# A two-layer block on one core: part of the RWKV chunks' transposes taken from products with the identity to TensorE's transpose mode

## The reference, cut to what matters

```python
def step(state, inp):
    r_t, w_t, k_t, v_t, kk_t, a_t = inp
    sa = jnp.einsum('bhij,bhj->bhi', state, -kk_t)
    state = (state * w_t[:, :, None, :]
             + sa[..., None] * (kk_t * a_t)[:, :, None, :]
             + v_t[..., None] * k_t[:, :, None, :])
    y_t = jnp.einsum('bhij,bhj->bhi', state, r_t)
    return state, y_t
_, ys = lax.scan(step, state0, xs)
```

## Time and profile before

| | before |
|---|---|
| median of 3 runs | 3451.0 us (3441.01 to 3458.84) |
| the profiled execution | 3451.66 us, its span 3449.9 us |
| TensorE matmul busy | 2585.6 us (75%), 17662 instructions |
| VectorE busy | 2055.5 us (60%) |
| GpSimd busy | 1353.6 us (39%) |
| ScalarE busy | 662.9 us (19%) |
| mean granted TensorE clock | 0.869 |
| HBM | 291 GB/s over the span |

### The profile page before, as it was taken

How to read it: one execution, slowest core, us unless ns; L and a number is a source line. 1 busy time by engine, 2 the same in 40 slices (tenths; PEclk the granted TensorE clock), 3 DMA queues, 4 the chain that set the end, 5 groups by cost and what they waited for, 6 DMA issues and landing times. The chain is left out here.

```text
span 3449.9 us, 44587 instructions
## 1 busy us (share of the span) xinstructions
PE 2585.6 (75%) x17662; PEld 1854.1 (54%) x17662; DVE 2055.5 (60%) x3910; ACT 662.9 (19%) x1414; POOL 1353.6 (39%) x1094
## 2 busy tenths in 40 slices
PE   6878563674887086888865657799999887977877
PEld 5767452562332075677753436477888676322222
DVE  6446989888764878999977987425232543000001
ACT  1122002211111013132222300132323422000001
POOL 0001476687877766777754666300000110000001
PEclk8989785886999597899987878999999898999998
DMA  8617798899999998999987799632343436999997
GB/s 332 207 37 244 251 324 301 305 385 352 343 369 401 390 340 313 329 399 398 398 337 275 262 362 354 219 98 87 114 118 95 147 113 231 426 428 428 428 429 302
DMA packets 391245, 1006.30 MB, mean 292 GB/s; under 512 B 30621, under 2 KB 234755, under 8 KB 375939
## 3 DMA queue, kind: packets, MB, share of 16 engines
q0 software_dynamic: 150912, 549.52, 42.4%
q1 hardware_dynamic: 207808, 405.44, 31.8%
q10 hardware_dynamic: 32323, 48.60, 3.9%
HBM read 971.99 MB, written 31.46 MB: 291 GB/s over the span
## 5 line engine op out<-in xcount | busy, mean ns | idle before, releaser
L1615 POOL DMA_INDIRECT ring<-in_peer_u_dram,index x512 | 691.6, 1351 | 338.6 <-DVE ring L1687 159.0
L1615 POOL DMA_INDIRECT ring<-in_peer_v_dram,index x512 | 613.1, 1197 | 274.6 <-issue 131.9
L352 PE MATMUL bank<-hT,weights 128*128 128x256 f32 x1984 | 448.4, 390 | 96.7 <-DVEq L149 46.6
L352 PEld LDWEIGHTS bank<-hT,weights 128*128 128x128 f32 x1984 | 387.7, 196 | 156.6 <-issue 99.8
L2008 PE MATMUL bank<-hT,weights 128*128 128x256 f32 x1792 | 424.6, 392 | 3.8 <-DVE weights L2211 3.3
L2008 PEld LDWEIGHTS bank<-hT,weights 128*128 128x128 f32 x1792 | 339.3, 194 | 55.2 <-DVE weights L2211 3.7
L1693 DVE SCALAR_TENSOR_TENSOR h_rows_b<-ring,coef,h_rows_b 128x1024 f32<-128x1024 f32 x238 | 305.2, 1282 | 50.4 <-DMA ring<-in_peer_v_dram,index 32.0
L1687 DVE SCALAR_TENSOR_TENSOR ring<-ring,h_rows_a 128x1024 f32<-128x1024 f32 x256 | 304.9, 1222 | 44.1 <-DMA ring<-in_peer_u_dram,index 41.5
L1687 DVE SCALAR_TENSOR_TENSOR ring<-ring,h_rows_b 128x1024 f32<-128x1024 f32 x256 | 299.9, 1223 | 8.1 <-DMA ring<-in_peer_u_dram,index 7.6
L1706 PE MATMUL bank<-ring,weights 128*128 128x512 f32 x512 | 239.2, 613 | 76.4 <-ACT weights L1728 50.2
L2797 POOL TENSOR_TENSOR sd_inn<-sd_inn,ssd_y 128x1024 f32<-128x1024 f32 x8 | 18.8, 2356 | 577.8 <-ACT sd_inn L2909 577.8
(11 more groups left out here) (579 smaller groups left out, 3965.2 us busy)
## 6 DMA issues: line engine op xcount, KB each, us to landing
weights<-in_w_in_dram SPq DMA_DIRECT2D x112, 512.0 KB, 4.1
weights<-in_w_in_dram SPq DMA_DIRECT2D x54, 1024.0 KB, 10.9
xp_near<-in_w_exp_gate_dram SPq DMA_DIRECT2D x9, 4096.0 KB, 34.4
xp_far<-in_w_exp_up_dram SPq DMA_DIRECT2D x9, 4096.0 KB, 32.9
xp_near<-in_w_exp_up_dram SPq DMA_DIRECT2D x7, 4096.0 KB, 33.9
xp_far<-in_w_exp_gate_dram SPq DMA_DIRECT2D x7, 4096.0 KB, 35.7
xp_far<-in_w_exp_down_dram SPq DMA_DIRECT2D x7, 4096.0 KB, 34.4
xp_near<-in_w_exp_down_dram SPq DMA_DIRECT2D x6, 4096.0 KB, 34.5
```

The lines of the kernel that those rows point to most:

```text
L352: ins = pe.matmul(m.ps[b][:, 0:TH], m.weights[:, s, k, c * P:(c + 1) * P], rhs(k), start=(k == 0), stop=(k == k_tiles - 1))
L1615: pool.indirect_dma_start(out=self.ring[:, n % RING, :], out_offset=None, in_=self.tables[table], in_offset=bass.IndirectOffsetOnAxis(ap=s ...
```

## The change

The three banks 5, 6 and 7 are no longer made by `heads` with the identity, but by a new helper `turned`. For each of the 8 tiles it turns the near head by `pe.transpose` (TensorE's transpose mode, with the identity as moving operand), and the far head by a matmul with the identity, as before. The order within a bank (near, far, near, far) and the semaphore at its end are the same, and so is everything else.

```diff
+        def turned(pe, bank, src):
+
+            for t in range(RT):
+                o, near, far = bank[:, t * RC:(t + 1) * RC], slice(0, RH), slice(RH, P)
+                pe.transpose(o[near], src[near, t, :], m.ident[near, near])
+                ins = pe.matmul(o[far], src[far, t, :], m.ident[far, far], start=True, stop=True)
+            return ins
+
...
-                    for b, l, rr in ((0, B, A), (1, A, B), (2, K, A),
-                                         (5, V, m.ident), (6, B, m.ident), (7, K, m.ident)):
+                    for b, l, rr in ((0, B, A), (1, A, B), (2, K, A)):
                         heads(pe, m.ps[b], (l, rr)).then_inc(made, 1)
+                    for b, src in ((5, V), (6, B), (7, K)):
+                        turned(pe, m.ps[b], src).then_inc(made, 1)
```

## The result

The changed kernel is slower: 3536.34 us median against 3448.18 us, a ratio of 1.0243 with a 95% interval of 1.0223 to 1.0264. It is outside the range on record, 3440 to 3484 us, on its slower side. (The median before is that of four runs here, hence 3448.18 and not the 3451.0 of the first three.)

A forecast was written before the change was run, and what follows sets the result against it. TensorE was taken to bound the second half's chunks, VectorE and full DMA engines the first half's. With near work hidden behind far matmuls, 24 x 0 = 0 left 3451 us, range 3440 to 3484 us.

The forecast's parts named there:

- What bounds the kernel, second half: Second half's four chunks: TensorE is busy without a gap, 85.40 of 85.40 us, so a microsecond on its list counts in full.
- The same, first half: First half's chunks: VectorE and DMA engines are full, so added TensorE time goes into 46.6 us of waiting for VectorE.
- Two streams, far sets the bank: Turned banks: near and far heads run side by side, and the unchanged far records keep a bank at 0.93 us.
- the transpose's price of 58 ns: Near heads in the turned banks: each 64 x 64 transpose takes 58 ns, bounds 54 and 109 ns, 0.46 us per bank.
- the sum of 0: All 24 turned banks: each stays at 0.93 us, as far matmuls hide the near work, so the change is worth 0.
- The switch of modes, priced at 0: Turned banks: going 16 times per bank between transpose and product costs nothing, judged from borders on the full array.
- The upper bound read from the change of the part in use: Borders between 64 x 64 banks and full-array work: 0.19 and 0.10 us, so a switch costs at most 0.29 us there and back.
- Rival 1: Turned banks: each pair drains the array, 0.35 us more, 33 us in the second half; 3484 us, up to 3518; chance 0.18.
- Rival 4: Turned banks: granted clock falls from 1.00 to 0.50, 3 us per chunk, 12 in the second half; 3463 us; chance 0.04.
- rival 2: Turned banks: each transpose takes the array alone for 58 ns without a drain, 5.6 us in all; 3457 us; chance 0.15.
- Rival 3: Turned banks: all records stand in one line of 29 ns each, saving 2.8 to 5.6 us; 3445 to 3448 us; chance 0.06.
- rival 5: Turned banks: a 64 x 64 transpose runs like a product, in two records, so nothing changes; 3451 us; chance 0.04.

The follow-up runs named there:

- the runs on sizes: Four pairs of transpose and product, of other sizes each time, added ahead of each bank's identity products in the kernel before: 3561.95, 3565.13, 3583.00, 3589.50 us, against 3527.53.

## Why the prediction was wrong, point by point

*What bounds the kernel, second half:* right. A microsecond on TensorE's list counted in full there (50 us worked out chunk by chunk, 49 in the stage, 50 in the run of that half alone, whose interval is 36 to 65).

*The same, first half:* wrong. The step "goes into 46.6 us of waiting" took a sum of TensorE's waits for a store of slack. The run of the first half alone gave 31 us (19 to 43). TensorE's two waits only went from 46.6 to 41.9 us, since they lie at other places of the chunk than the lateness, and VectorE, the engine that sets the time there, got a new wait of 45.3 us in place of 3.4.

*Two streams, far sets the bank:* right as a reading of the kernel before (0.93 us with the near products alone), and so was the transpose's price of 58 ns (56 measured). But the sum of 0 hung on the words "if the two streams stay independent", and they don't.

*The switch of modes, priced at 0:* this is the step that failed. It went by the borders on the full array, and these hold, even for single instructions (0.33 us a pair). The upper bound read from the change of the part in use, 0.29 us there and back, was the right row to take: 0.25 to 0.26 us in five readings. The argument that "a 64 x 64 transpose needs no other part of the array than its product did" is contradicted by the runs on sizes: it drains against a product of its own size (0.43 us) and not against one on all 128 columns (0.28 us), as if it used them all. So in place of 0.93 us a bank took 8 x 0.43 = 3.4 us at full clock.

*Rival 1, drain at every transpose:* this is what happened, and the runs agree with the mechanism named: the array's arrangement is left and taken up again for each pair. Its pair was to cost 0.35 us more, and costs 0.31 at full clock. Its 33 us for the second half are 24 x 4 x 0.31 = 30 us. I had given it 0.18, which was too little for a bound that came from a row of this kernel. Two terms were missing from its 3484 us: the first half's 31 to 35 us, which it sent into the waiting, and the clock. Its other figure, 3518 us with nothing hidden, had the first and lacked the second.

*Rival 4, the clock:* set up as an alternative to rival 1, though here the two came together. In the last chunk the clock fell from 1.00 to 0.50 in the banks, 5 us after their start, and came back 6 us after the spare work began, as in the earlier trace rows. It took 5.3 us there against the 3 forecast, and about 20 of the second half's 50 us: those that the 30 us of pairs leave. With the same transposes in groups the clock stayed at 1.00, so that a bare count of transposes doesn't bring it down. It stayed at 1.00 too (2480 to 2760 us) in the last two of the four runs on sizes, which drain too, with 12 draining pairs per chunk among the banks of products. What it is in 24 pairs in a row that brings it down stays open.

*Rivals 2, 3 and 5:* rival 2 had the end of the side by side right, which makes a bank of 24 x 0.058 = 1.39 us; the grouped bank's 1.63 is this and one drain. Rival 3 is ruled out by the near products alone (0.93 us with 16 records), rival 5 by the count of 17470 instructions.

*A row misread:* the 124 ns for a record of a full product are 112, as said above. Nothing in the sum hung on it.

Put together for the two profiled executions, the 84.4 us are 30 (drains, second half), about 20 (clock, second half) and 35 (first half, both causes together). The 20 and the 35 are what is left of measured sums, so this is an account and not a second test; the test is the pair of runs with one half each, 31 and 50 us.

*The two rules of the Trainium skill* ("TensorEngine Tiling (Array Packing)": column tiling excludes the float32 transpose mode; a change of tiling mode drains the engine) were cited in the prediction and not followed. The changed kernel and the four runs on sizes agree with the two taken together, with the drain at 0.25 to 0.26 us for there and back.

## What to carry to other kernels

Before an operation is put in among others, ask whether it changes the array's division and count the changes in the order of the program: here each pair of them cost 0.25 us, four times the transpose itself, and put an end to two streams that ran side by side. Going by these runs, take a float32 transpose as one that uses all columns; put it in a group of its own or beside products on all columns and the same rows. Waits summed over a stage are no reserve: look at whether the engine that sets the time waits, at the place where the lateness will arrive, and read the granted clock and the distance of starts, not the busy share.

## What the runs showed of the hardware that was not expected

- A float32 transpose on 64 rows and 64 columns runs without a drain among products on 64 rows and 128 columns (0.28 us a pair), and with one among products of 64 x 64 (0.43 us, without it 0.17).
- A drain also parts transpose and product of one and the same 64 x 64 part (0.43 us).
- At half the clock the drain doesn't double. A pair takes 0.64 us there, and less three records of 0.107 us (one of 16 in a bank at half clock) 0.32 us are left, against 0.26 at full clock.
- TensorE was shown as busy 4.00 of 4.00 us while the clock was taken down to 0.50, with 20 records in that time.
